# One more K group of the first projection pass multiplied as split weights and activations (hybrid encoder layer, one core)

## The chip, the cores and the metric

The kernel runs on one core of a Trainium2 chip. The metric is the device time of one execution in microseconds (us). The core's engines run their own instruction streams and meet at semaphores: TensorE (PE, with its weight loads shown as PEld), VectorE (DVE), ScalarE (ACT), GpSimd (POOL) and the sync engine SP, which only issues transfers here. POOL issues transfers too. All transfers share 16 DMA engines.

## The reference, cut to what matters

One encoder layer on x (1, 256, 2048), float32, with conditioning vector c (1, 2048). The part that the change touches is the beginning:

```python
c_act = jax.nn.silu(c)
mod = c_act @ w_mod[l] + b_mod[l]                     # (1, 6*2048), w_mod is 2048 x 12288
sh1, sc1, gt1, sh2, sc2, gt2 = [m[:, None, :] for m in jnp.split(mod, 6, axis=-1)]
h = x * (1.0 + sc1) + sh1
proj = h @ w_in[l]                                    # 2048 x 5764 columns
```

proj feeds four groups of heads: RWKV-7 time mixing (r, k, v and three low-rank inputs), an indexer with sparse attention, band attention, and retention. Their outputs are mixed by w_out, normalised, modulated, and go through a gated MLP with a depthwise convolution (w_up, w_down) and a second normalisation. The result is (1, 256, 2048), float32.

## The kernel before, in words

**Tiling.** K = 2048 is 16 tiles of 128. w_in is read in chunks of 512 KB (1024 float32 elements on each of 128 partitions) into `RAW`, a ring of four buffers, by SP. The chunk number n counts through the whole kernel; `N0_OUT` = 96 chunks belong to w_in. A chunk n uses buffer n % 4 of `RAW`, and of `WHI` and `WLO` where it is split.

**Two ways of multiplying.** A split chunk is copied by ACT from RAW to WHI in the reduced type fp32r (`split_hi`, L507 to L521), DVE writes the remainder RAW - WHI to WLO (`split_lo`, L805 to L816), and PE makes three products for each tile of 128 x 128 weights: WHI with HHI, WHI with HLO, WLO with HHI (`fm`). HHI and HLO are the same split of the modulated activations h. A chunk that isn't split ("native") is multiplied as float32 straight from RAW, with the float32 activations in `XT`: 8 products, which the trace shows as 16 matmul records, two each. Which way a chunk goes is decided by `n < WHOLE`, in `split_hi`, `split_lo`, `w_in_half` (PE, L1432 and L1442) and in SP's release of a buffer (L398). Before the change `WHOLE` is 28.

**The first pass.** The modulation `mod` isn't known at the start, so the kernel computes it in parts of 1024 columns: POOL streams 16 tiles of w_mod for each part into `MODR` and `MODA` (a ring of eight buffers for the first four parts, then of four, MODR alone), and DVE multiplies and accumulates them into `ACC` (`mod_add`, L833 and L836). Part g holds the shift and scale of K tiles 4g to 4g+3. PE sums a part over the partitions (`mod_reduce`, 16 records), DVE adds the bias (`mod_cols`, L844), makes h in XT for the four K tiles (`h_new_tile`, L875), ACT copies them to HHI (L546), DVE makes HLO (`h_split`, L868). So the first pass goes through K in four groups (`GROUPS`), each of seven chunks (`GROUP_CHUNKS`): two of the K block, one "lora" chunk (two tiles wide, four K tiles deep), two of the R block, two of the V block. Chunks 0 to 6 are group 0, 21 to 27 group 3. All seven accumulators stay in PSUM: K and R in banks G, V and lora in banks M. Chunks 28 to 31 (QI block) and all later ones were split before the change already.

**Order of the work.** Every engine's order is written out. DVE, for each group g: first tile of part g+1, `mod_cols(g)`, four `h_new_tile`, second tile of part g+1, four `h_split`; then for g < 3 the other 14 tiles of part g+1, and behind each odd tile t a `split_lo(7g + t//2 - 1 + 3)`, which does nothing for a chunk under WHOLE. In g = 2 that is chunk 21 behind tile 11, chunk 22 behind tile 13, chunk 23 behind tile 15. ACT, before the HHI copies of K tile 12: `split_hi` of chunks 17 to 23. From n = 21 on DVE, ACT and PE follow a loop over n in two halves: DVE does a tile of w_mod and then `split_lo(n + 3)` (`AHEAD` = 3), ACT does `split_hi(n + 3)`, PE multiplies chunk n, and a table `SETUP` puts small steps between: "squares" at n = 23 and "norms" at n = 24 (PE sums squares, ACT takes roots), "inverse 0" to "inverse 3" on DVE at n = 25, 25, 26, 27, "lora" on PE at n = 29, "cumulate" on DVE at n = 30. Behind the last chunk of a block ACT and DVE take its accumulators out (`evac_in`): block K behind n = 22, lora behind 23, R behind 25, V behind 27.

**Waits that matter.** PE's native chunk waits for its RAW buffer and for h_new of its K tiles; a split chunk waits for `lo_done` and for all 16 HLO tiles (`h_lo`). ACT writes a WHI buffer only when PE has used the chunk four before. SP reloads a RAW buffer when PE has used it (native chunk) or when DVE has made its remainder (split chunk). At n = 24 SP issues five constant loads first (L389 to L393), at n = 26 it waits for all 16 HLO tiles and loads `LNAB`, then goes on. POOL issues tile q of w_mod when DVE has finished tile q - 4 (in the ring of eight tile q - 8); tile 64 (part 4, tile 0) is therefore issued behind tile 60.

Of the kernel before, what the change touches and what calls it, by code (L numbers as in the profile page):

```python
# [71 lines left out]
GROUPS = 4  # L72
GROUP_CHUNKS = 7
FIRST_CHUNKS = (GROUPS - 1) * GROUP_CHUNKS
MODS_BESIDE_H = 2
WHOLE = GROUPS * GROUP_CHUNKS
K_BLOCK, R_BLOCK, V_BLOCK, QI_BLOCK, LORA = 0, 1, 2, 3, "lora"
A_TILES = {K_BLOCK: 4, LORA: 12, R_BLOCK: 0, V_BLOCK: 8}

# [88 lines left out]
def encoder_layer(nc, x, c, w_mod, b_mod, w_in, rwkv_mu, rwkv_w0, rwkv_w2, rwkv_a0, rwkv_a2, rwkv_g2,  # L168
# [96 lines left out]
    with ExitStack() as ctx:  # L265
# [46 lines left out]
        def raw_count(n):  # L312

            double = sum(1 for m in range(n % RING, n + 1, RING) if m // CH_IN == 5)
            return 16 * (n // RING + 1 + double)
# [35 lines left out]
        def _(sp):  # L351
# [32 lines left out]
            for n in range(N0_OUT):  # L384
# [12 lines left out]
                if n >= RING:  # L397
                    sp.wait_ge(w_used if n - RING < WHOLE else lo_done, n - RING + 1)  # L398
                at = 0
# [107 lines left out]
        def _(act):  # L507
            def split_hi(n):

                if n < WHOLE or n >= N_ALL:  # L510
                    return
# [19 lines left out]
            act.activation(CSG, CCOL, ACT.Sigmoid).then_inc(silu_c, 1)  # L531
            act.activation(SM[:, 220:221], CCOL[:, 0:1], ACT.Copy).then_inc(hi_done, WHOLE)
            for g, (dst, n) in enumerate([(PCOL[:, 0:122], 122), (PCOL[:, 128:248], 120), (BMC[:, :], 96)]):
# [259 lines left out]
        def _(dve):  # L793
            own = [0, None]

            def mark(ins):

                own[0] += 1
                return ins.then_inc(dve_own, 1)

            def settle():

                dve.wait_ge(dve_own, own[0] if own[1] is None else own[1] + own[0])

            def split_lo(n):  # L805

                if n < WHOLE or n >= N_ALL:
                    return
# [45 lines left out]
            mark(dve.tensor_tensor(CC, CCOL, CSG, ALU.mult))  # L854
            dve.tensor_copy(SM[:, 221:222], CCOL[:, 0:1]).then_inc(lo_done, WHOLE)
            settle()
# [518 lines left out]
        def _(pe):  # L1375
# [51 lines left out]
            def w_in_half(n, half):  # L1427
# [3 lines left out]
                if half == 0:  # L1431
                    if n < WHOLE:  # L1432
                        pe.wait_ge(raw_in[s], raw_count(n))
# [432 lines left out]
```

## Time and profile before

| | |
|---|---|
| runs of the kernel, us | 1432.05, 1434.29, 1435.09 (median 1434.29) |
| the profiled execution's own time, us | 1434.29 |
| its span, us | 1432.5 |
| TensorE, busy share | 93% |
| VectorE, busy share | 68% |
| ScalarE, busy share | 38% |
| mean granted TensorE clock | 0.973 of full |
| moved by DMA | 318.98 MB, mean 223 GB/s |

The span runs from the first to the last instruction of the profiled execution; its own time lies 1.8 us above it. Busy shares are means over stages with different limits, so they don't say what bounds a given stage. The first pass over K groups is the stretch from about 40 to 165 us of the span; in it the DMA engines move 374 to 399 GB/s most of the time, well above the kernel's mean.

### The profile page before, as it was taken

What the parts mean: (1) busy time and instruction counts of PE and PEld (TensorE: products, weight loads), DVE (VectorE), ACT (ScalarE), POOL (GpSimd) and SP (SyncE); (2) the same over time, 40 slices, a digit from 0 to 9 for tenths busy, and PEclk for the clock granted to TensorE, in tenths of its full rate; (3) what the DMA queues carried; (4) which work ended last, traced back from release to release, by engine and by line L of the source; (5) the groups of instructions that cost most, each with busy time, mean ns of one, the idle gap of its engine ahead of it and who ended that gap; (6) DMA issues with size and microseconds to landing.
All of it is one profiled execution on the core that took longest, in us unless ns stands there. A gap on an engine that the chain in (4) does not pass through costs nothing.

```text
span 1432.5 us, 23097 instructions
## 1 busy us (share of the span) xinstructions
PE 1331.2 (93%) x8833; PEld 1211.6 (85%) x8833; DVE 975.0 (68%) x1266; ACT 538.7 (38%) x765; POOL 158.4 (11%) x223
## 2 busy tenths in 40 slices
PE   1989879999899999997999999999999999999994
PEld 1878779889797677787999999999999998888883
DVE  5776787787779877658877787556555554545545
ACT  1000533332433434434444343534444453333331
POOL 4332111101011111002710100000000000000001
PEclk9899999999999999998999999999999999999997
DMA  9999875666567665763587877555565647665561
GB/s 358 385 384 374 299 274 166 221 189 199 160 203 265 214 198 207 278 202 105 172 278 254 303 249 256 176 170 183 176 188 164 204 152 228 245 195 191 183 199 59
DMA packets 142879, 318.98 MB, mean 223 GB/s; under 512 B 12142, under 2 KB 19680, under 8 KB 141792
## 3 DMA queue, kind: packets, MB, share of 16 engines
q1 hardware_dynamic: 114528, 213.23, 45.6%
q0 software_dynamic: 28288, 104.89, 21.0%
q8 instruction: 42, 0.69, 0.2%
q14 instruction: 21, 0.17, 0.0%
HBM read 315.98 MB, written 2.10 MB: 222 GB/s over the span
## 4 chain that ended last, share of the span: by engine, by line
PE 74%; DVE 14%; DMA 8%; issue 2%; ACT 1%; POOL 0%; DVEq 0%; SPq 0%; ACTq 0%; POOLq 0%
PE G L1377 65%; PE M L1377 8%; DVE ACC L836 5%; DMA MODA<-in_w_mod_dram 5%; DVE WLO L816 2%; DMA RAW<-in_w_in_dram 2%; DMA RAW<-in_w_out_dram 1%; PE M L1541 0%; ACT WHI L521 0%; DVE SC L1113 0%; DVE X L1361 0%; DVE X L1370 0%; DVE SM L1111 0%; PE M L1645 0%; DVE SM L1125 0%
## 5 line engine op out<-in xcount | busy, mean ns | idle before, releaser
L1377 PE MATMUL G<-HHI,WHI 128*128 128x256 f32 (+1 forms) x1744 | 503.8, 289 | 0.0
L1377 PE MATMUL G<-HLO,WHI 128*128 128x256 f32 (+1 forms) x1744 | 495.8, 284 | 0.0
L1377 PE MATMUL G<-HHI,WLO 128*128 128x256 f32 (+1 forms) x1744 | 495.7, 284 | 0.0
L1377 PEld LDWEIGHTS G<-HHI,WHI 128*128 128x128 f32 (+1 forms) x1744 | 336.4, 193 | 4.3 <-issue 3.7
L1377 PEld LDWEIGHTS G<-HLO,WHI 128*128 128x128 f32 (+1 forms) x1744 | 336.4, 193 | 0.5 <-issue 0.5
L1377 PEld LDWEIGHTS G<-HHI,WLO 128*128 128x128 f32 (+1 forms) x1744 | 335.9, 193 | 0.0
L816 DVE TENSOR_TENSOR WLO<-RAW,WHI 128x1024 fp32r<-128x1024 f32 x182 | 221.2, 1222 | 165.5 <-ACT WHI L521 161.8
L821 DVE TENSOR_TENSOR WLO<-RAW,WHI 128x1024 fp32r<-128x1024 f32 x174 | 217.6, 1270 | 140.1 <-ACT WHI L527 140.0
L521 ACT ACTIVATE WHI<-RAW 128x1024 fp32r<-128x1024 f32 x182 | 192.0, 1059 | 206.3 <-PE G L1377 168.5
L527 ACT ACTIVATE WHI<-RAW 128x1024 fp32r<-128x1024 f32 x174 | 179.9, 1054 | 185.2 <-PE G L1377 151.1
L836 DVE SCALAR_TENSOR_TENSOR ACC<-MODR,SM,ACC 128x1024 f32<-128x1024 f32 x118 | 150.7, 1277 | 17.2 <-DMA MODR<-in_w_mod_dram 14.7
L1377 PE MATMUL G<-WHI,FHI 128*128 128x512 f32 x352 | 136.9, 389 | 0.0
L1377 PE MATMUL G<-WLO,FHI 128*128 128x512 f32 x352 | 136.9, 389 | 0.0
L1377 PE MATMUL G<-WHI,FLO 128*128 128x512 f32 x352 | 136.9, 389 | 0.0
L1377 PE MATMUL G<-WHI,HHI 128*128 128x512 f32 x224 | 92.6, 413 | 2.9 <-DVE WLO L816 2.9
L455 POOL DMA_DIRECT2D MODR<-in_w_mod_dram x96 | 50.9, 530 | 357.6 <-DVE ACC L836 333.3
L1377 PE MATMUL G<-WHI,HLO 128*128 128x512 f32 x224 | 88.2, 394 | 0.0
L1377 PE MATMUL G<-WLO,HHI 128*128 128x512 f32 x224 | 87.6, 391 | 0.0
L1377 PEld LDWEIGHTS G<-WHI,FLO 128*128 128x128 f32 x352 | 66.1, 188 | 13.8
L1377 PEld LDWEIGHTS G<-WHI,FHI 128*128 128x128 f32 x352 | 66.1, 188 | 13.8
L1377 PEld LDWEIGHTS G<-WLO,FHI 128*128 128x128 f32 x352 | 66.1, 188 | 13.5
L1377 PE MATMUL G<-XT,RAW 128*128 128x256 f32 x256 | 63.3, 409 | 7.6 <-DVE XT L875 4.5
(276 smaller groups left out, 1385.0 us busy)
## 6 DMA issues: line engine op xcount, KB each, us to landing
RAW<-in_w_up_dram SPq DMA_DIRECT2D x176, 512.0 KB, 4.4
MODR<-in_w_mod_dram POOLq DMA_DIRECT2D x160, 512.0 KB, 5.8
RAW<-in_w_in_dram SPq DMA_DIRECT2D x88, 512.0 KB, 5.9
RAW<-in_w_down_dram SPq DMA_DIRECT2D x88, 512.0 KB, 4.3
MODA<-in_w_mod_dram POOLq DMA_DIRECT2D x32, 512.0 KB, 13.8
RAW<-in_w_out_dram SPq DMA_DIRECT2D x32, 512.0 KB, 4.7
X<-in_x_dram SPq DMA_DIRECT2D x2, 1024.0 KB, 9.3
XR<-in_x_dram POOLq DMA_DIRECT2D x2, 1024.0 KB, 8.5
```

What stands on the lines that cost most here:

```text
L455: pool.dma_start(MODR[:, t % RING, :], wm[:, t, ds(m * MOD_W, MOD_W)])\
L521: act.activation(WHI[:, s, :, :], RAW[:, s, :, :], ACT.Copy).then_inc(hi_done, 1)
L527: act.activation(WHI[:, s, :, :], RAW[:, s, :, :], ACT.Copy).then_inc(hi_done, 1)
L816: dve.tensor_tensor(WLO[:, s, :, :], RAW[:, s, :, :], WHI[:, s, :, :].bitcast(f32), ALU.subtract).then_inc(lo_done, 1)
L821: dve.tensor_tensor(WLO[:, s, :, :], RAW[:, s, :, :], WHI[:, s, :, :].bitcast(f32), ALU.subtract).then_inc(lo_done, 1)
L836: ins = dve.scalar_tensor_tensor(a, w, ck, a, ALU.mult, ALU.add)
L1377: return pe.matmul(out_, l, r, start=start, stop=stop, skip_group_check=True)
```

## The change

`WHOLE` becomes `FIRST_CHUNKS`, which is 21. Chunks 21 to 27, the last K group of the first pass, are then split by ACT and DVE and multiplied by PE in three products, with HHI and HLO of K tiles 12 to 15, which both kernels make anyway for the later blocks. Groups 0 to 2 stay native. The three counters that start at WHOLE (`hi_done`, `lo_done`) start at 21 accordingly, and SP's release of buffers 21 to 27 is by `lo_done`. No order of instructions is rewritten; calls of `split_hi` and `split_lo` that did nothing for chunks 21 to 27 now do their work where they stand.

```diff
@@ -73,7 +73,7 @@
 GROUP_CHUNKS = 7
 FIRST_CHUNKS = (GROUPS - 1) * GROUP_CHUNKS
 MODS_BESIDE_H = 2
-WHOLE = GROUPS * GROUP_CHUNKS
+WHOLE = FIRST_CHUNKS
 K_BLOCK, R_BLOCK, V_BLOCK, QI_BLOCK, LORA = 0, 1, 2, 3, "lora"
 A_TILES = {K_BLOCK: 4, LORA: 12, R_BLOCK: 0, V_BLOCK: 8}
```

## Rows read from the trace of the kernel before

**Rows 1.** The chain that ended last, from 90 us: start, us, what.
```profile
129.76 19.18 DMA RAW<-in_w_in_dram
148.98 3.73 PE G L1377 x16
152.73 6.29 DMA RAW<-in_w_in_dram
...
160.13 1.22 DVE WLO L816
```
**Rows 2.** VectorE in order of time: start us, us, what [idle before it, what ended it].
```profile
121.73 1.28 DVE L836 SCALAR_TENSOR_TENSOR ACC<-MODR,SM,ACC 128x1024 f32<-128x1024 f32 x1 [0.97 <-DMA MODR<-in_w_mod_dram]
...
129.80 1.28 DVE L836 SCALAR_TENSOR_TENSOR ACC<-MODA,SM,ACC 128x1024 f32<-128x1024 f32 x1 [0.74 <-DMA MODA<-in_w_mod_dram]
...
133.33 1.38 DVE L875 TENSOR_SCALAR XT<-XT,MC 128x256 f32<-128x256 f32 x4
135.96 1.28 DVE L836 SCALAR_TENSOR_TENSOR ACC<-MODR,SM,ACC 128x1024 f32<-128x1024 f32 x1 [1.25 <-DMA MODR<-in_w_mod_dram]
137.16 1.43 DVE L868 TENSOR_TENSOR HLO<-XT,HHI 128x256 fp32r<-128x256 f32 x4
...
143.95 1.65 DVE L903 SCALAR_TENSOR_TENSOR PA<-G,PCOL,PA 128x255 f32<-128x255 f32 x4 [0.60 <-ACT PA L555]
...
154.23 0.43 DVE L920 TENSOR_SCALAR RN<-RN 128x512 f32<-128x512 f32 x1 [4.07 <-ACT RN L597]
...
160.13 1.22 DVE L816 TENSOR_TENSOR WLO<-RAW,WHI 128x1024 fp32r<-128x1024 f32 x1 [1.72 <-ACT WHI L521]
...
172.30 1.55 DVE L903 SCALAR_TENSOR_TENSOR PA<-M,PCOL,PA 128x255 f32<-128x255 f32 x4
173.78 2.66 DVE L836 SCALAR_TENSOR_TENSOR ACC<-MODR,SM,ACC 128x1024 f32<-128x1024 f32 x2
```
**Rows 3.** TensorE in order of time, same columns.
```profile
36.03 3.57 PE L1377 MATMUL M<-CFT,ACC 128*128 128x1 f32 x16 [9.44 <-DVE ACC L836]
...
131.14 1.95 PE L1377 MATMUL M<-CFT,ACC 128*128 128x1 f32 x16 [1.41 <-DVE ACC L836]
134.21 8.83 PE L1377 MATMUL G<-XT,RAW 128*128 128x256 f32 x32 [1.12 <-DVE XT L875]
...
154.26 3.62 PE L1377 MATMUL G<-XT,RAW 128*128 128x256 f32 x16
157.72 7.07 PE L1377 MATMUL M<-XT,RAW 128*128 128x256 f32 x32
164.64 0.36 PE L1377 MATMUL G<-HHI,WHI 128*128 128x256 f32 x1
...
170.35 0.28 PE L1377 MATMUL G<-HHI,WLO 128*128 128x256 f32 x1
173.96 2.48 PE L1377 MATMUL M<-PA,W2A 64*128 64x256 f32 x16 [3.33 <-DVE PA L903]
```
**Rows 4.** The load into RAW issued between 117.5 and 121 (chunk 21): issue, and landing.
```profile
L402 SPq DMA_DIRECT2D RAW<-in_w_in_dram x1: 368/368/368, 119.4 to 119.4; - x1
...
DMA to landing us min/median/max: 9.9/9.9/9.9
```
**Rows 5.** ScalarE in order of time, columns as in Rows 2: the first copy into WHI.
```profile
159.04 1.06 ACT L521 ACTIVATE WHI<-RAW 128x1024 fp32r<-128x1024 f32 x1 [3.98 <-DMA RAW<-in_w_in_dram]
```
**Rows 6.** MODR's loads issued at 125.6 and at 133.6: time from issue to landing.
```profile
DMA to landing us min/median/max: 6.5/6.5/6.5
...
DMA to landing us min/median/max: 10.6/10.6/10.6
```
**Rows 7.** Stretches: us, busy (x) of PE PEld DVE ACT POOL, PEclk, DMA share, GB/s.
```profile
40.70:46.00 5.30, 5.28 (x13) 4.29 (x14) 5.20 (x9) 0.97 (x4) 1.44 (x2) 0.54 1.05 381
134.20:136.00 1.80, 1.79 (x5) 1.44 (x6) 0.55 (x3) 0.96 (x3) 0.00 (x0) 0.55 1.02 362
129.76:164.64 34.88, 29.89 (x136) 25.70 (x137) 21.82 (x33) 11.38 (x23) 4.79 (x9) 0.95 0.95 333
164.64:202.71 38.07, 26.99 (x199) 25.38 (x199) 37.48 (x48) 19.98 (x34) 7.93 (x15) 0.91 0.89 320
```

## The prediction, made before the changed kernel ran

> **What bounds the kernel now.** The page's busy shares name TensorE as the engine of the whole, but the change lies in one stage, so I read the chain of waits first, in the stretch from 90 us on. There it does not stay on TensorE: it shows the 19.18 us load of chunk 24, issued when chunk 20 frees its buffer at 129.76, then chunk 24, then the 6.29 us load of chunk 28, and at 160.13 it goes over to VectorE [rows 1]. The windows confirm it: from 129.76 to 164.64 VectorE is busy 21.82 of 34.88 us while the DMA engines are 95% busy, and from 164.64 to 202.71 VectorE is busy 37.48 of 38.07 us and TensorE only 26.99 [rows 7]. So the first stretch has slack on VectorE and none on the transfers; the second has none on VectorE. TensorE waits 3.33 us there, until 173.96, for VectorE's evacuation of block V, which begins at 172.30 [rows 2, 3]. Whatever arrives late on VectorE at about 160 us arrives late at the end; whatever TensorE saves before is idle time unless VectorE is early too.
>
> **TensorE's own gain.** A native chunk costs 157.72 - 154.26 = 3.46 us from start to start. A split one: two chunks are 48 records from 164.64 to 170.35, or 0.1215 us from one to the next, 24 x 0.1215 = 2.92 us [rows 3]. Seven chunks save 7 x 0.54 = 3.8 us of TensorE. I count none of it, because VectorE's order covers it; if that cover were gone the whole 3.8 us would be gain.
>
> **VectorE's and ScalarE's added work.** Seven copies of 1.06 us on ScalarE [rows 5] and seven remainders of 1.22 us on VectorE [rows 2]: 7.4 and 8.5 us. By busy time alone both fit into the 34.88 - 21.82 = 13 us that VectorE is idle between 129.76 and 164.64 [rows 7]. By position three of them do not: those for chunks 21, 22 and 23 stand between tiles of w_mod part 3, before the summing on which group 3's activations hang.
>
> **Step A, the stall before part 3 is complete.** VectorE finishes tile 11 at 121.73 + 1.28 = 123.0 [rows 2]. The next instruction is now the remainder of chunk 21. Its load is issued at 119.4, when TensorE has used chunk 17, and takes 9.9 us: it lands at 129.3 [rows 4]. ScalarE stands at this copy with nothing before it, so it is done 1.06 us later [rows 5], at 130.4, and the remainder at 131.6. Queued behind the waiting instruction are tiles 12 to 15, all of them landed by 129.80 [rows 2]. They now run at 2.66 us for two [rows 2], with the remainder of chunk 22 between: 131.6 + 2.66 + 1.2 + 2.66 = 138.1, where before tile 15 ended at 131.1. That is +7.0 us. Chunk 22 does not add to it: issued one native chunk (3.5 us) behind 21, by the same 9.9 us it lands at 132.8 and is copied before 134.2.
>
> **Step B, the sum over part 3.** TensorE has nothing else from 129.7 on, now for 8.4 us instead of 1.41 [rows 3]. The same 16 records took 1.95 us behind 1.41 us of idleness and 3.57 us behind 9.44 [rows 3]; I take the latter, +1.6. The sum ends at 141.7 (before 133.1). Meanwhile VectorE does the remainder of chunk 23 (issued two native chunks behind 21, at 126.3, landed by the same 9.9 us at 136.2 and copied at 137.3; done 139.3) and tile 64. POOL issues tile 64 one step behind tile 60, now at 133.6 instead of 125.6; the landing times here are 6.5 to 10.6 us [rows 6]. With 6.5 it is there at 140.1 and hidden under the sum; with 10.6 it is there at 144.2 and, with the tile's own work (under 1 us), adds 3.2 us. I take the low end, since the four slots refill from an empty queue as tile 64 did at 125.6, and keep the other for the range.
>
> **Step C, the new wait for HLO.** A native chunk needed only h_new; chunk 21 now waits for all HLO tiles. The bias and h_new end 1.6 us behind the sum (134.71 against 133.09 before), so at 143.3; tile 65 takes another 1.2 and the four subtractions 1.43 [rows 2]: 145.9 against 138.6 before for the same point, +7.3. It is not the full 8.6 because tile 65's old wait of 1.25 us for its transfer [rows 2] is gone. TensorE's group 3 starts at 145.9 instead of 134.21 [rows 3].
>
> **Step D, TensorE from cold.** The two chunks at 134.21 took 8.83 us where the warm pair at 157.72 needs 6.92; the clock in that stretch was granted at 0.55, which is mostly the 1.2 GHz level, behind 4.5 us with little work [rows 3, 7]. In group 0, behind 9.44 us of idleness, the granted clock was 0.54 for the first 5.3 us [rows 7], a loss of some 2.6 us. Here TensorE did even less before. I take the mean of 1.9 and 2.6: 2 x 2.92 + 2.3 = 8.1 us, chunk 22 ends at 154.0, chunk 23 at 156.9, chunk 24 at 159.9.
> The Trainium skill, page "TensorE: Matmul & The Clock Gate", section "HAM oscillation — how this bites in real kernels", says that a gap in the matmuls throws TensorE back to the slow clock and that the cold stretch costs half its length; that speaks against this change, which lengthens such a gap. By that rule steps B and D cost what I have put down; without it they would cost nothing and the sum would be about 3.9 us lower. The trace agrees, with the two clock rows just named.
>
> **Step E, the evacuations behind it.** Block K's evacuation ended 2.6 us behind chunk 22 before (145.60 against 143.04) [rows 2, 3], so now at 156.6. VectorE then does tile 68 and the remainder of chunk 26 (159.0), waits for ScalarE, which has chunk 26's copy of 1.06 us more than before in front of its squares and lora copies, evacuates lora (160.1), does tile 69 and the remainder of chunk 27 (162.5). The first root came 1.7 us behind chunk 24 before (154.23 against 152.5) [rows 1, 2]; now, behind lora's evacuation, by 161.8. So the normalisation starts at 162.5 where it started at 154.23: +8.2. It is VectorE's two added remainders and TensorE's late start together that make the 0.9 us over step C.
>
> **Step F, what is given back.** Before, VectorE waited 1.72 us for chunk 28's copy at 160.13 [rows 2], because its buffer was freed only by TensorE at 152.73 [rows 1]. Now the buffer is freed by the remainder of chunk 24 at about 148, so the wait is gone; with the smaller overlaps around it I give back 2.0. From there VectorE is back to back as before. Block V's evacuation starts at 178.5 instead of 172.3, TensorE's lora step follows it, and everything behind is the same order with the same durations.
>
> **Sum,** as the delay against before at each point: +7.0 at the end of part 3 (A), +8.6 at the end of its sum (B), +7.3 at HLO (C), +8.2 at the normalisation (D, E), and with the 2.0 given back (F) **+6.2 us** from there to the end. The profiled execution took 1434.29 us, the same as the median of the runs, so the forecast is 1440.5 us. The transfers get no term: the bytes are the same, chunk 24 lands before it is needed, and LNAB with chunk 26, issued behind HLO at about 147, has until 155 to land. The bounds: with B and D at no clock loss +2.3; with tile 64 landing 10.6 us after issue +9.4.
>
> **Rivals.**
> (1) The transfers come late in convoy. Behind the stall, tile 64 and later chunk 26 meet the five constant loads in the queues; then the high end holds in both places, +9.4 us, 1443.7. For it: chunk 24 needed 19.18 us [rows 1]. Against: POOL's queue is empty for about 4 us, and this lets SP's drain. Chance 0.13.
> (2) The shift is absorbed. VectorE's loop behind 160 us has tiles of w_mod that could run in any gap, and the attention stages behind 200 us have TensorE at work; if a later wait is for something not delayed, the 6.2 us shrink to 0 to 2.5 us: 1434.3 to 1436.8. For it: VectorE is only 68% busy over the span. Against: all later steps are chained to this one in fixed order, with nothing that waits for an absolute time. Chance 0.14.
> (3) Faster. The load of chunk 21 is on time. If buffers landed within 3.6 us of their issue (123.0 - 119.4) the three remainders would fill gaps of 0.7 to 1.0 us before the tiles [rows 2]; SP would free RAW earlier, the wait for chunk 24 (2.49 us, from 146.5 to 148.98 [rows 1]) and the one of 1.72 us [rows 2] would vanish: 1434.3 - 4.2 = 1430.1. It decides at that landing time. Against: 9.9 us measured, with the transfers saturated. Chance 0.08.
> Beside this rival stands the Trainium skill's page "FP8 and Floating Point Precision", section "TensorE Precision Notes": true FP32 takes four passes. By that, three products would save a quarter, 7 x 0.87 = 6.1 us instead of the rows' 3.8, and a TensorE-bound stage would end near 1428. The rows disagree in size (0.1215 us per product), not in direction.
> That the change does not do what it says has next to no chance: the constant is read in all four places.
>
> **Chances and range.** The forecast has 0.65, by itself 1437 to 1443. A measurement of this kernel can tell about 0.2%, 2.9 us, from no change. Slower by more than that (above 1437.2): nearly all of the forecast and rival 1, and a little of rival 2, 0.77. Within: 0.15. Faster: 0.08. The range of 1435.2 to 1444 leaves out rival 3 and part of 2.
>
> **What would show it.** Step A: VectorE idle some 7 us from 123.0, ended by ScalarE's copy of chunk 21, and tile 15 ending near 138. B: the 16 records at 3.0 to 3.6 us. C: the first split matmul of group 3 near 146, released by HLO. D: chunks at 2.92 us once warm. F: no wait for chunk 28, and TensorE's lora step 5 to 7 us later than 173.96. The prediction is wrong if VectorE doesn't wait at chunk 21, or if that step is late and the end is not.

## The result: slower, by the mechanism forecast and by less

The changed kernel took 1438.41 us (median of 18 runs, 1434.82 to 1440.16), the kernel before 1433.96 us (18 runs, 1431.58 to 1439.74). The medians differ by 4.45 us. The ratio estimated from all these runs is 1.0024, 95% interval 1.0014 to 1.0035: 3.4 us slower, between 2.0 and 5.0. A second session, with 7 runs of the changed kernel, gave 1.0036 (1.0018 to 1.0054). The profiled execution took 1438.44 us with a span of 1436.5 (before 1434.29 and 1432.5).

The page of the changed kernel: busy time of the engines, then the two largest groups that changed.
```profile
PE 1329.6 (93%) x8889; PEld 1213.4 (84%) x8889; DVE 983.5 (68%) x1273; ACT 546.0 (38%) x772; POOL 158.5 (11%) x223
...
L1377 PE MATMUL G<-HHI,WHI 128*128 128x256 f32 x1776 | 513.2, 289 | 4.3 <-DVE HLO L868 4.3
...
L816 DVE TENSOR_TENSOR WLO<-RAW,WHI 128x1024 fp32r<-128x1024 f32 x189 | 229.7, 1222 | 174.7 <-ACT WHI L521 171.1
```
VectorE and ScalarE have exactly seven instructions more (189 remainders against 182). TensorE is less busy by 1.6 us and yet the kernel is slower, so its busy time doesn't tell what this stage waits for.

VectorE of the changed kernel in order of time (start us, us, what [idle before it, what ended it]), to be read against [rows 2]:
```profile
121.73 1.28 DVE L836 SCALAR_TENSOR_TENSOR ACC<-MODR,SM,ACC 128x1024 f32<-128x1024 f32 x1 [0.83 <-DMA MODR<-in_w_mod_dram]
130.92 1.22 DVE L816 TENSOR_TENSOR WLO<-RAW,WHI 128x1024 fp32r<-128x1024 f32 x1 [7.90 <-ACT WHI L521]
132.06 2.67 DVE L836 SCALAR_TENSOR_TENSOR ACC<-MODA,SM,ACC 128x1024 f32<-128x1024 f32 x2
...
135.78 2.67 DVE L836 SCALAR_TENSOR_TENSOR ACC<-MODA,SM,ACC 128x1024 f32<-128x1024 f32 x2
...
141.05 0.75 DVE L833 TENSOR_SCALAR ACC<-MODR,SM 128x1024 f32<-128x1024 f32 x1 [1.47 <-DMA MODR<-in_w_mod_dram]
...
144.82 1.42 DVE L868 TENSOR_TENSOR HLO<-XT,HHI 128x256 fp32r<-128x256 f32 x4
...
153.04 1.23 DVE L816 TENSOR_TENSOR WLO<-RAW,WHI 128x1024 fp32r<-128x1024 f32 x1 [3.27 <-ACT WHI L521]
155.76 1.65 DVE L903 SCALAR_TENSOR_TENSOR PA<-G,PCOL,PA 128x255 f32<-128x255 f32 x4 [1.49 <-ACT PA L555]
...
163.03 0.92 DVE L920 TENSOR_SCALAR RN<-RN 128x512 f32<-128x512 f32 x2
...
166.76 1.22 DVE L816 TENSOR_TENSOR WLO<-RAW,WHI 128x1024 fp32r<-128x1024 f32 x1
...
178.92 1.56 DVE L903 SCALAR_TENSOR_TENSOR PA<-M,PCOL,PA 128x255 f32<-128x255 f32 x4
```
Tile 11 of part 3 starts at 121.73 in both traces. Then VectorE stands 7.90 us at the remainder of chunk 21, and tiles 12 to 15 run behind it in two pairs, with the remainder of chunk 22 between them. HLO is 7.7 us late, block K's evacuation 11.8, the normalisation 8.8, block V's evacuation 6.6. The 3.27 us in front of the remainder of chunk 25 (153.04) are a wait for a free WHI buffer: ScalarE can copy that chunk only when TensorE has used chunk 21. It ends before TensorE is done with chunk 22 at 154.8, for which block K's evacuation waits, so it is covered.

TensorE of the changed kernel, against [rows 3], and the granted clock of the sum and of the first chunk (columns as in [rows 7]):
```profile
138.50 3.57 PE L1377 MATMUL M<-CFT,ACC 128*128 128x1 f32 x16 [8.17 <-DVE ACC L836]
146.39 0.55 PE L1377 MATMUL G<-HHI,WHI 128*128 128x256 f32 x1 [4.32 <-DVE HLO L868]
...
180.58 3.79 PE L1377 MATMUL M<-PA,W2A 64*128 64x256 f32 x16 [3.33 <-DVE PA L903]
```
```profile
138.50:142.10 3.60, 3.57 (x16) 3.48 (x16) 1.84 (x2) 0.00 (x0) 0.53 (x1) 0.50 1.03 406
146.40:151.90 5.50, 5.50 (x26) 5.50 (x27) 3.37 (x3) 0.00 (x0) 1.06 (x2) 0.50 0.91 231
151.90:154.80 2.90, 2.90 (x25) 2.90 (x25) 1.23 (x1) 1.06 (x1) 0.00 (x0) 0.98 1.05 416
```

**What was not forecast: half of the delay disappears later.** I set the two traces side by side instruction by instruction, leaving the seven added remainders out. VectorE's cumulate step (L939, 184.93 before) is 7.2 us late. Then the delay falls for good at two places only: to 5.7 at the update of DI at 209.54, and to 3.9 at the one at 266.88. Both are places where VectorE waits for TensorE. The windows there, first of the kernel before, then of the changed kernel, shifted by its delay of about 7.2 and 5.5 us:
```profile
202.60:206.00 3.40, 3.29 (x15) 3.29 (x16) 3.19 (x7) 0.00 (x0) 0.00 (x0) 0.51 0.68 229
260.70:264.00 3.30, 3.30 (x19) 3.30 (x17) 3.27 (x10) 0.00 (x0) 0.00 (x0) 0.50 0.63 254
```
```profile
209.90:213.20 3.30, 3.30 (x29) 3.30 (x29) 3.27 (x6) 0.00 (x0) 0.00 (x0) 0.98 0.71 210
266.20:269.50 3.30, 3.30 (x32) 3.30 (x31) 3.27 (x10) 0.00 (x0) 0.00 (x0) 1.00 0.81 325
```
The kernel before ran these two stretches at 1.2 GHz, the changed kernel at 2.4 GHz: 3.4 us at half speed is 1.7 us of work lost, and the waits of VectorE behind them are 1.69 and 1.81 us in the kernel before, 0.50 and 0.26 in the changed one. Whether that is the change's doing or the draw of one execution is asked below.

### The profile page after: what moved, and what is told of

The parts are those of the page before. It is cut to its first block, busy times and chain, and to the rows that moved or that the text cites. A ratio compares the mean times of both kernels' runs of the same rounds, so it can differ in the third digit from the quotient of the medians.

```text
span 1436.5 us, 23223 instructions
## 1 busy us (share of the span) xinstructions
PE 1329.6 (93%) x8889; PEld 1213.4 (84%) x8889; DVE 983.5 (68%) x1273; ACT 546.0 (38%) x772; POOL 158.5 (11%) x223
## 4 chain that ended last, share of the span: by engine, by line
PE 74%; DVE 15%; DMA 7%; issue 3%; ACT 1%; POOL 0%; DVEq 0%; POOLq 0%; SPq 0%; ACTq 0%
PE G L1377 65%; PE M L1377 8%; DVE ACC L836 5%; DMA MODA<-in_w_mod_dram 5%; DVE WLO L816 2%; DMA RAW<-in_w_out_dram 1%; DMA RAW<-in_w_in_dram 1%; PE M L1541 0%; ACT WHI L521 0%; DMA MODR<-in_w_mod_dram 0%; DVE SC L1113 0%; DVE RN L924 0%; DVE X L1361 0%; DVE X L1370 0%; DVE SM L1111 0%
## 5 line engine op out<-in xcount | busy, mean ns | idle before, releaser
L1377 PE MATMUL G<-HHI,WHI 128*128 128x256 f32 x1776 | 513.2, 289 | 4.3 <-DVE HLO L868 4.3
L1377 PE MATMUL G<-HLO,WHI 128*128 128x256 f32 x1776 | 505.2, 284 | 0.0
L1377 PE MATMUL G<-HHI,WLO 128*128 128x256 f32 x1776 | 505.0, 284 | 0.0
L1377 PEld LDWEIGHTS G<-HHI,WHI 128*128 128x128 f32 x1776 | 342.6, 193 | 8.6 <-issue 7.4
L816 DVE TENSOR_TENSOR WLO<-RAW,WHI 128x1024 fp32r<-128x1024 f32 x189 | 229.7, 1222 | 174.7 <-ACT WHI L521 171.1
L1377 PEld LDWEIGHTS G<-HLO,WHI 128*128 128x128 f32 x1776 | 342.8, 193 | 0.5 <-issue 0.5
L1377 PEld LDWEIGHTS G<-HHI,WLO 128*128 128x128 f32 x1776 | 342.5, 193 | 0.0
L821 DVE TENSOR_TENSOR WLO<-RAW,WHI 128x1024 fp32r<-128x1024 f32 x174 | 218.4, 1275 | 139.2 <-ACT WHI L527 139.0
L521 ACT ACTIVATE WHI<-RAW 128x1024 fp32r<-128x1024 f32 x189 | 199.4, 1059 | 232.4 <-PE G L1377 178.1
L527 ACT ACTIVATE WHI<-RAW 128x1024 fp32r<-128x1024 f32 x174 | 180.0, 1054 | 185.2 <-PE G L1377 144.9
L836 DVE SCALAR_TENSOR_TENSOR ACC<-MODR,SM,ACC 128x1024 f32<-128x1024 f32 x118 | 150.7, 1277 | 13.7 <-DMA MODR<-in_w_mod_dram 11.2
L503 POOL TENSOR_TENSOR X<-X,LN2B 128x1024 f32<-128x1024 f32 x2 | 6.6, 3306 | 548.2 <-DVE X L1368 548.2
```

The costliest lines, as they stand in the source:

```text
L503: pool.tensor_tensor(X1[:, 1, cols], X1[:, 1, cols], LN2B[:, cols], ALU.add).then_inc(out_ready[1], 1)
L521: act.activation(WHI[:, s, :, :], RAW[:, s, :, :], ACT.Copy).then_inc(hi_done, 1)
L527: act.activation(WHI[:, s, :, :], RAW[:, s, :, :], ACT.Copy).then_inc(hi_done, 1)
L816: dve.tensor_tensor(WLO[:, s, :, :], RAW[:, s, :, :], WHI[:, s, :, :].bitcast(f32), ALU.subtract).then_inc(lo_done, 1)
L821: dve.tensor_tensor(WLO[:, s, :, :], RAW[:, s, :, :], WHI[:, s, :, :].bitcast(f32), ALU.subtract).then_inc(lo_done, 1)
L836: ins = dve.scalar_tensor_tensor(a, w, ck, a, ALU.mult, ALU.add)
```

## The experiments

Landmarks of every trace, read off VectorE's rows, and each timing against the kernel before on the same chip. A landmark is the start of the same instruction in each trace, in us of the span: tile 15 of w_mod part 3, the subtractions that make HLO, the evacuation of block K (K out), the normalisation (norms), the cumulate step, the update of DI that is at 266.88 in the kernel before, and a late one at 834.5. Some kernels were timed in different sessions, so two ratios with overlapping intervals are not told apart.
```
kernel             tile 15   HLO    K out  norms  cumulate  DI(266.9)  834.5   ratio to before (95%)
before               129.8  137.2  143.9  154.2   184.9      266.9     834.5
before, again        130.3  137.9  145.8  153.8   185.7      266.2     835.4
changed              137.2  144.8  155.8  163.0   192.1      270.8     838.4   1.0024 (1.0014 to 1.0035)
changed, again       136.9  144.6  154.3  161.6   190.2      272.4     838.5   1.0036 (1.0018 to 1.0054)
late_split           129.8  137.1  152.0  159.9   191.8      275.8     841.9   1.0015 (1.0004 to 1.0026)
stall_only           132.8  142.1  150.2  157.7   188.6      271.0     840.2   1.0023 (1.0007 to 1.0039)
whole24              130.5  137.8  153.2  161.1   190.8      271.3     839.0   1.0056 (1.0036 to 1.0077)
late_const           130.4  137.6  148.3  155.6   185.2      264.1     829.7   0.9982 (0.9964 to 1.0000)
late_const_again     130.0  137.6  147.7  155.0   185.8      269.4     835.8   0.9987 (0.9975 to 0.9999)
before_const         130.1  136.2  144.3  151.8   186.3      268.9     838.1   1.0014 (1.0001 to 1.0028)
after_const          137.2  144.8  154.9  162.1   192.1      272.5     838.6   1.0046 (1.0029 to 1.0062)
warm_gap2            137.1  145.3  154.5  161.8   191.5      271.9     839.1   1.0033 (1.0020 to 1.0047)
```

**1. The same work, elsewhere in VectorE's order (late_split).**
```diff
                     for n in range((kt // 4 - 1) * GROUP_CHUNKS, kt // 4 * GROUP_CHUNKS):
-                        split_hi(n + AHEAD)
+                        if n + AHEAD < FIRST_CHUNKS + 2:
+                            split_hi(n + AHEAD)
                 act.wait_ge(h_new, kt + 1)
                 act.activation(HHI[:, kt, :], XT[:, kt, :], ACT.Copy).then_inc(h_hi, 1)
+            split_hi(FIRST_CHUNKS + 2)
...
-                        if t % 2:
+                        if t % 2 and g * GROUP_CHUNKS + t // 2 - 1 + AHEAD < FIRST_CHUNKS:
                             split_lo(g * GROUP_CHUNKS + t // 2 - 1 + AHEAD)
...
                     h_new_tile(kt)
+                if g == GROUPS - 1:
+                    split_lo(FIRST_CHUNKS)
                 mod_add(g + 1, 1)
                 for kt in range(4 * g, 4 * g + 4):
                     h_split(kt, 0)
+                if g == GROUPS - 1:
+                    split_lo(FIRST_CHUNKS + 1)
+                    split_lo(FIRST_CHUNKS + 2)
```


> The changed kernel with the same seven split chunks, but VectorE's remainders of chunks 21, 22 and 23 moved out of the accumulation of w_mod part 3: chunk 21 behind h_new of K tiles 12 to 15, chunks 22 and 23 behind the HLO tiles; ScalarE's copy of chunk 23 moved behind its HHI copies. My theory (the place of the three remainders costs the time, not their work): VectorE does not wait at chunk 21, tile 15 of part 3 ends near 131 instead of 138, HLO is complete near 139, TensorE starts group 3 near 139 to 140, and the normalisation starts near 156 (before: 154.2, changed: 163.0). End 0 to 2 us above the kernel before. Rival (the 8.5 us of added VectorE work costs it): the work is unchanged, so the end stays 3.5 to 4.5 us above the kernel before.

The median was 2.8 us above the kernel before (1435.68 against 1432.88), ratio 1.0015 (2.2 us), so the end lies between the two forecasts (0 to 2, and 3.5 to 4.5); the profiled execution was the slowest of its twelve, so I read its landmarks only up to the cumulate step. The first half came as my theory had it: no wait at chunk 21, tile 15 at 129.8, HLO at 137.1, as in the kernel before. The second half did not: the norms came at 159.9, not 156. VectorE of this kernel:
```profile
138.44 2.35 DVE L818 TENSOR_TENSOR WLO<-RAW,WHI 128x1024 fp32r<-128x1024 f32 x2
140.71 1.28 DVE L838 SCALAR_TENSOR_TENSOR ACC<-MODR,SM,ACC 128x1024 f32<-128x1024 f32 x1
148.52 1.22 DVE L818 TENSOR_TENSOR WLO<-RAW,WHI 128x1024 fp32r<-128x1024 f32 x1 [6.53 <-ACT WHI L521]
```
Three chunks further the same thing waits: the remainder of chunk 24, in front of a tile of w_mod and of block K's evacuation, for a load that is issued at 130.0 behind the five constants and lands 17.4 us later. In the changed kernel the same load, behind the same five constants, lands 10.2 us after its issue at 130.4, well before VectorE reaches it. There POOL issues no load of w_mod between 115.7 and 134.0, because VectorE stands still and frees no buffer; in late_split POOL goes on issuing. So the stall at chunk 21 both made VectorE late for chunk 24 and coincided with an early landing. Neither theory got it whole.

**2. Only the last four chunks split (whole24).**
```diff
-WHOLE = FIRST_CHUNKS
+WHOLE = FIRST_CHUNKS + 3
```


> Only chunks 24 to 27 are split (WHOLE = 24), 21 to 23 stay native: no remainder stands inside the accumulation of part 3 and group 3 starts at h_new as before, while four copies and four remainders and the new release of buffers stay. My theory: part 3 ends near 131 and group 3 starts near 134 as before; chunk 24 lands near 149, is split by 151.4 and multiplied by 154.3 (before 152.5); the wait for chunk 28 goes. End -1 to +1.5 us against before. Rival (work): 4/7 of the measured +3.4, so about +2 us.

A miss for both: 1.0056 (6 runs), where at most about 2 us was expected. That it is worse than splitting all seven is not shown: its interval overlaps that of the changed kernel's second session, and at the cumulate step it stands at 190.8, between the changed kernel's two traces. Fewer added instructions, and again a long wait:
```profile
149.76 1.23 DVE L816 TENSOR_TENSOR WLO<-RAW,WHI 128x1024 fp32r<-128x1024 f32 x1 [9.04 <-ACT WHI L521]
```
I had followed chunk 24 on TensorE (split by 151.4) and forgotten what stands behind its remainder on VectorE: block K goes out at 153.2 instead of 143.9, though TensorE was done with it at 144.7, and TensorE then stands 4.17 us before the norms for the lora block.

**3. Only the wait (stall_only).**
```diff
+                        if (g, t) == (GROUPS - 2, 11):
+                            dve.wait_ge(raw_in[FIRST_CHUNKS % RING], raw_count(FIRST_CHUNKS))
                         if t % 2:
```
This is the kernel before with that one wait; no chunk more is split.

> The kernel before (chunks 21 to 27 native, no split work added) with one wait added on VectorE: behind tile 11 of w_mod part 3 it waits until chunk 21 has landed. Nothing else waits for it. My theory: VectorE idles from 123.0 to about 129.3, catches up on tiles 12 to 15 at 1.33 us each and ends part 3 near 134.7 (+3.6 us against before), TensorE's sum takes about 3.6 us instead of 1.95 because TensorE has idled longer, h_new is done near 140 (+5); the native chunks start without waiting for HLO. Of that some 1.7 us comes back at VectorE's wait for chunk 28. End +1 to +3.5 us. Rival (added work alone is the cause): end within 0.5 us of the kernel before.

```profile
128.61 5.45 DVE L836 SCALAR_TENSOR_TENSOR ACC<-MODA,SM,ACC 128x1024 f32<-128x1024 f32 x4 [5.21 <-DMA RAW<-in_w_in_dram]
138.77 0.75 DVE L833 TENSOR_SCALAR ACC<-MODR,SM 128x1024 f32<-128x1024 f32 x1 [4.71 <-DMA MODR<-in_w_mod_dram]
```
1.0023, and +3.7 us at the cumulate step, as my theory had it. A wait on VectorE without a single added arithmetic instruction costs half or more of what the changed kernel loses there (+7.2 and +5.2 in its two traces), and in the time of the whole kernel it can't be told from the changed kernel (1.0024). The second row shows one way in which the stall is passed on: tile 64 of w_mod is issued only when VectorE has freed a buffer, so it is late too, and VectorE stands another 4.71 us for it. The rival (added work alone) falls.

**4. The constants behind chunk 27, on both kernels and on late_split.**
```diff
-                if n == FIRST_CHUNKS + 3:
+                if n == FIRST_CHUNKS + 7:
                     sp.dma_start(CBT[:, :], const_b.bitcast(bf16)).then_inc(late_in, 16)
```


> The kernel of the run late_split (changed kernel, remainders of chunks 21 to 23 moved behind h_new and HLO) with the five constant loads (1.6 MB) moved from ahead of chunk 24 to ahead of chunk 28 in SP's queue. In late_split VectorE stood 6.5 us at chunk 24, which landed only at 147.4. My theory (in the split version the place of a remainder in VectorE's order makes it wait for the landing of its chunk: first 21, then 24): chunk 24 now lands before 142, VectorE does not wait there, block K is taken out from about 148 (late_split 152.1), the normalisation starts near 156 (before 154.2, late_split 159.9). End within 1.5 us of the kernel before, and 2 us or more below late_split. Rival (added work decides): as late_split, +2 us.

> The kernel before with only the constant loads moved to ahead of chunk 28. Control for late_const, and a version that could beat both. My theory: chunk 24 lands before TensorE wants it at 146.5, the wait of 2.49 us goes, chunk 24 ends near 150, chunk 28 is loaded 2.5 us earlier; VectorE's normalisation starts near 151.7 instead of 154.2 and the end is 1.5 to 3.5 us below the kernel before. Rival (the bytes are only moved within a saturated stretch): the wait comes back at chunk 28, end unchanged.

> The changed kernel with only the constant loads moved to ahead of chunk 28. My theory: in the changed kernel chunk 24 is not waited for (the stall at chunk 21 covers its landing), so nothing is gained: end within 1 us of the changed kernel, +3 to +4.5 us against before. Rival (the constants ahead of chunk 24 are part of the loss here too): 2 us or more below the changed kernel.

late_const: ratio 0.9982, median 1429.99 us against 1433.97. Chunk 24 lands 10.2 us after its issue at 129.2, its remainder has no wait, the norms start at 155.6 (expected near 156). VectorE carries all seven added remainders in the stretch where it had been idle; the windows to compare with [rows 7]:
```profile
129.76:164.64 34.88, 26.55 (x192) 25.91 (x192) 29.29 (x39) 18.73 (x31) 4.75 (x9) 0.85 1.02 362
164.64:202.71 38.07, 27.33 (x198) 25.77 (x198) 37.46 (x48) 18.84 (x33) 7.93 (x15) 0.91 0.83 293
```
29.29 us busy instead of 21.82 in the first, and the cumulate step at 185.2, 0.3 us behind the kernel before. So the work of the change, put behind the data that it needs, costs nothing up to there.

before_const: ratio 1.0014, so the constants' place alone is no gain, and the rival was nearer. The norms did start at 151.8 (expected 151.7), but chunk 28 now stood behind the constants, landed 9.8 us after its issue at 150.3 and was waited for 5.21 us where the kernel before waited 1.72 [rows 2]:
```profile
161.22 1.23 DVE L816 TENSOR_TENSOR WLO<-RAW,WHI 128x1024 fp32r<-128x1024 f32 x1 [5.21 <-ACT WHI L521]
```
In late_const RAW buffers 21 to 27 are freed by VectorE and not by TensorE, so chunk 28 is asked for at 145.6; it takes 13.7 us and lands at 159.3, only 0.8 us earlier. Its wait is short, 1.02 us, mostly because VectorE gets there later.

after_const: no gain, as my theory had it, with the changed kernel's landmarks to 1 us: where the stall at chunk 21 stays, chunk 24's landing is covered. The forecast of the end was missed, though: 1.0046 is +6.6 us (4.2 to 8.9) against +3 to +4.5. No landmark shows why, and the interval overlaps that of the changed kernel's second session. One thing did change in its trace, tile 64 of w_mod:
```profile
139.54 0.75 DVE L833 TENSOR_SCALAR ACC<-MODR,SM 128x1024 f32<-128x1024 f32 x1
142.15 0.17 DVE L844 TENSOR_TENSOR MC<-M,BMC 128x8 f32<-128x8 f32 x1 [1.86 <-PE M L1377]
```
It landed 4.7 us after its issue instead of 7.0, and VectorE then waited 1.86 us for the slow sum instead; HLO came at the same time (144.8).

**5. TensorE kept busy through the gap (warm_gap2).**
```diff
+                    if m == GROUPS - 1:
+                        pe.wait_ge(mod_col, m)
+                        for _ in range(34):
+                            mm(M[3][:, 256:384], IDENT, ONES, start=True, stop=True)
...
+                        if n == FIRST_CHUNKS:
+                            pe.wait_ge(mod_col, GROUPS)
+                            for _ in range(14):
+                                mm(M[3][:, 256:384], IDENT, ONES, start=True, stop=True)
```


> The changed kernel with idle TensorE time filled by products that nobody reads (34 products of 128x128 float32 ahead of the sum of part 3, 14 more between the modulation columns and chunk 21), into an unused part of a PSUM bank. My theory: the granted clock stays at full through the gap; the sum's 16 records take about 1.9 instead of 3.57 us and chunks 21 and 22 take 5.8 instead of 8.4, so VectorE's normalisation comes 2 to 4 us earlier than in the changed kernel (near 160 instead of 163) and the end is 1 to 3 us below the changed kernel's, as far as later clock episodes don't take it back. Rival (VectorE's chain decides, the clock costs nothing here): the end is as in the changed kernel.

The clock did what was expected, the time hardly. The sum and the tile of VectorE that runs beside it:
```profile
138.44 1.95 PE L1377 MATMUL M<-CFT,ACC 128*128 128x1 f32 x16 [0.36 <-DVE ACC L836]
```
```profile
141.92 0.75 DVE L833 TENSOR_SCALAR ACC<-MODR,SM 128x1024 f32<-128x1024 f32 x1 [2.39 <-DMA MODR<-in_w_mod_dram]
```
The sum took 1.95 us instead of 3.57 and ended at 140.4. But VectorE's next instruction, tile 64 of w_mod, was waited for until 141.92, and HLO came at 145.3 (changed kernel 144.8). Together with after_const this shows two things that end at nearly the same moment: with tile 64 early the slow sum holds VectorE, with the sum fast tile 64 does. Each was taken away alone; both together were not. Behind it chunks 21 and 22 took 6.0 us (147.57 to 153.57) instead of 8.5, but the 14 dummy products ran until 147.8 and held chunk 21 up by some 0.7 us after HLO was complete. The norms came at 161.8 against 163.0, which is no gain beyond the draw: the changed kernel's second trace, with the slow clock, has them at 161.6. The ratio 1.0033 lies among the changed kernel's own, although the granted clock of these 12 runs was 0.972 in the mean, as in the kernel before, and 0.969 in the 18 runs of the changed kernel. The clock was not kept at full throughout either: from 142.8 to 147.0, with only the second batch running, it was granted at 0.59.

**6. The same kernels once more.**

> The kernel before, unchanged, for a second trace. In the first pair of traces the changed kernel was 7.2 us late at VectorE's cumulate step (182.6 us of the span) and only 3.9 us late behind 267 us; the difference lay where the kernel before had two stretches of 3.4 us at half the granted clock (202.6 and 260.7) and the changed kernel none. Theory 1 (the position of the half-clock stretches is chance from one execution to the next): in this trace the time from 182.6 us to the end differs from that of the first by one or more steps of about 1.7 us. Theory 2 (it belongs to the order of the instructions): the same stretches at the same places, within 0.5 us.

> The changed kernel, unchanged, for a second trace and a second timing beside late_const_again. Up to VectorE's cumulate step the trace should repeat: wait of 7 to 8 us at chunk 21, part 3 complete near 138.5, +7 us at that step. Behind it, theory 1 (chance of the half-clock stretches): another end by steps of about 1.7 us. Theory 2: half-clock stretches and the give-back of 3.3 us as in the first trace. Time +3 to +5 us against before.

> The kernel of late_const once more, on whatever chip this is, since its interval reached from 0.9964 to 1.0000. If the gain is real the ratio is again 0.997 to 0.999; if it was the draw of clock stretches, within 0.1% of the kernel before. Its trace stood 0.3 us behind the kernel before at the cumulate step, so what gain there is must come from behind 200 us.

Up to HLO everything repeats within 0.8 us (wait at chunk 21: 7.61 us). Behind that it does not. From the cumulate step to the landmark at 834.5 the first trace of the changed kernel gives back 3.2 us, the second gets from +5.2 to +6.8 at 373 us (380.1 against 373.3) and is at +4.0 at the landmark as well. late_const gains 5.1 us on that way in one trace and loses 0.5 in the other. The kernel before, traced again, gains 1.5 us and loses 1.6 again between 500 and 600 us, so the steps of theory 1 show inside that way, while the whole of it differs by 0.2 us only. (The cumulate step starts at 184.93; the 182.6 in the expectation is a slip.) The two traces of the kernel before at the first of the two places, the update of DI:
```profile
209.54 0.69 DVE L1007 TENSOR_TENSOR DI<-M,DI 128x512 f32<-128x512 f32 x1 [1.69 <-PE M L1377]
208.85 0.69 DVE L1007 TENSOR_TENSOR DI<-M,DI 128x512 f32<-128x512 f32 x1 [0.44 <-PE M L1377]
```
In all twelve traces this wait is either 1.69 to 1.99 us (before, late_split, late_const_again) or 0.43 to 0.50 us (the other nine), and the three with the long wait are those in which a half-clock stretch of 3.4 us begins 6 to 7 us ahead of the step. Both kinds occur with the kernel before and with late_const, whose instructions are identical in both traces. The half-clock stretches behind 200 us lie in other places or last longer or shorter each time: the changed kernel had none between 210 and 322 us in the first trace and two in the second, of 3.4 us at 251.4 and of 10.2 us at 265.0. So theory 1: the give-back in the first pair was mostly the draw, its first half that of the first trace of the kernel before. late_const_again gives the gain once more, smaller (0.9987, interval 0.9975 to 0.9999), in one session with the changed kernel's 1.0036 (1.0018 to 1.0054).

## Why the prediction was right, and where its size was off

**Step A** held. The wait was 7.90 us, ended by ScalarE's copy, with chunk 21 landing 9.8 us after its issue (9.9 used). Tiles 12 to 15 ended at 138.4 against 138.1 forecast, +7.4 against +7.0. late_split shows that it is this place and not the work: HLO returned to 137.1. stall_only shows that the bare wait suffices for half of the delay or more.

**Step B** had the right numbers (sum 3.57 us, h_new from 142.3) and a claim that no run bears out: that without the slow clock the sum of B and D would be 3.9 us lower. warm_gap2 took the slow clock from the sum and TensorE's first chunks and moved the norms by 1.3 us, no more than the changed kernel's own two traces differ. I had bounded tile 64's landing at 6.5 to 10.6 us and called it hidden by the slow sum; it took 7.0 and was level with it, so taking away the one leaves the other. What the slow clock costs where tile 64 is early no run shows.

**Step C** held: the first split product at 146.39 (forecast 145.9), released by HLO, the one idle entry that the page newly shows for TensorE.

**Step D** held: from the first of the 48 products to chunk 23 8.3 us (146.39 to 154.68, forecast 8.1), the first 5.5 us at granted clock 0.50. Its working had a slip: 5.3 us at 0.54 are a loss of 2.4 us, not 2.6, which moves the forecast by 0.1 us. The Trainium skill, page "TensorE: Matmul & The Clock Gate", section "HAM oscillation — how this bites in real kernels", says that a gap in the matmuls throws TensorE back to the slow clock, and this stretch agrees, with 0.50 granted behind the gap. That it decides the time of this kernel, which I drew from it, warm_gap2 does not bear out.

**Steps E and F** held to a microsecond: norms 163.0 (162.5), no wait for chunk 28, block V out from 178.9 (178.5), TensorE's lora step 180.58 against 173.96, +6.6 in the range of 5 to 7 that I named. Averaged over two traces of each kernel the cumulate step is at 191.2 against 185.3, +5.9; the forecast was +6.2.

**What was off in size** is the end of step F, the sentence that "everything behind is the same order with the same durations". The order is the same; the durations are not, since the stretches of slow clock change place from one execution to the next. One stretch of 3.4 us at half clock is 1.7 us if it lies on the path, and of the first pair's 7.2 us two such stretches took 3.3 back. Over many runs the loss is 3.4 us (2.0 to 5.0), in the second session 5.2 (2.6 to 7.7). The forecast of +6.2 lies above the first interval and inside the second; that the time itself, 1438.41, fell into the range was helped by a range of nearly 9 us. Rival 2 had named such an absorption, but for gaps on VectorE; in the first pair it came through TensorE's clock. How much of the 5.9 us at the cumulate step is given back on average, and not by the draw, is open. The twelve traces hint that some is: from the cumulate step to the landmark at 834.5 the eight traces of kernels with added split chunks gain 1.8 us in the mean against the first trace of the kernel before (from a gain of 5.1 to a loss of 0.6), and the four with chunks 21 to 27 native lose 1.1 (0 to 2.2). I sorted them so only after seeing them, and no run was made to test it.

**Rival 3** had the right condition (chunk 21 in time, or rather nobody waiting for it) and an incomplete price: with it met in late_split, chunk 24 took over. Only with both removed does the kernel gain, by 0.13 to 0.18%, with intervals that end at 0.9999 and 1.0000. That late_const is faster although its cumulate step is at par with the kernel before stays open, and goes with the hint above: behind that step its instructions are the same.

## What to carry to other kernels

A helper that does nothing for some chunks marks places where nobody has asked yet whether the data has landed. Turning it on puts a wait there, and on an engine that works in order the wait is paid by what stands behind it: so look up the landing time of each load against the time at which its first consumer is reached, on that consumer's engine. Counting busy time would have passed this change (8.5 us into 13 us of idleness); the work did fit once the remainders stood behind the landings. Removing one wait shows the next one (chunk 21, then 24; in before_const 24, then 28), so test a repair on the landmark before which nothing else is late, and judge a change of 0.2% by many runs, since here two stretches of half clock are as large as the effect.

## What the runs showed of the hardware

- The places and lengths of the half-clock stretches behind 200 us differ between executions of one kernel (one of 3.4 us at 202.6 us in one trace of the kernel before, none there in the other). In the first pair they lasted 3.4 to 17.1 us up to 400 us of the span. A stretch of 3.4 us just ahead of the update of DI goes with a wait of 1.69 to 1.99 us there, and its absence with one of 0.43 to 0.50. 18 runs of the changed kernel spread over 5.3 us.
- A 512 KB load took 9.8 us to land with the DMA engines fully busy. Behind five constant loads (1.6 MB) in the same queue it took 17.4 to 19.2 us where POOL went on loading w_mod, and 10.2 us in the changed kernel, where POOL issued no such load between 115.7 and 134.0. It also took 10.2 us where the constants were moved behind it.
